# Band attention beside the convolution's products in the mixer of a first block, its values computed by token

## The reference, cut to what matters

```python
def first_block(x, ...):
    x = x + 0.5 * swiglu(rms_norm(x, ffn1_norm[l]), ...)
    h = rms_norm(x, mix_norm[l])
    proj = h @ w_in[l]                      # 1024 -> 3*512 + 512 + 8 + 8 + 3*512
    qkv_a, z_a, a_a, b_a, qkv_b = jnp.split(proj, split_at, axis=-1)
    o_a = gdn_mixer(qkv_a, z_a, a_a, b_a, conv_w[l], a_log[l], dt_bias[l], gdn_norm_w[l])
    o_b = dilated_mixer(qkv_b, q_norm_w[l], k_norm_w[l], rel_bias)
    x = x + jnp.concatenate([o_a, o_b], axis=-1) @ w_out[l]
    ...
def gdn_mixer(qkv, z, a, beta_logit, ...):
    qkv = jax.nn.silu(short_conv(qkv, conv_w))          # 5 taps along the tokens
    q, k, v = l2_normalize(qkv[0]), l2_normalize(qkv[1]), qkv[2]
    ...                                                 # delta rule, forward and backward
    o = rms_norm(o, norm_w) * jax.nn.silu(z)
def dilated_mixer(qkv, q_norm_w, k_norm_w, rel_bias):   # 8 heads of 64
    q = rms_norm(qkv[:, :, 0], q_norm_w) * (SWA_HEAD_DIM ** -0.5)
    k = rms_norm(qkv[:, :, 1], k_norm_w)
    v = qkv[:, :, 2]
    ...   # three dilations: band softmax of q k + bias, merged by their log sums
```

## Time and profile before

| | us |
|---|---|
| median of 3 runs (2813.7 to 2827.72) | 2822.07 |
| profiled execution | 2823.88 |
| its span | 2822.1 |
| PE busy in the span | 2644.0 (94%) |
| DVE busy | 1724.8 (61%) |
| ACT busy | 1046.6 (37%) |
| share of PE in the chain that ended last | 88% |

### The profile page before, as it was taken

One profiled execution on the slowest core, in us unless ns is written; L12 is line 12 of the kernel. 1 busy time (PEld: TensorE's weight loads), 2 busy tenths in 40 slices (PEclk: granted clock), 3 DMA queues, 4 the chain that ended last, 5 costly groups with the idle time before them and its releaser, 6 DMA issues.

```text
span 2822.1 us, 37400 instructions
## 1 busy us (share of the span) xinstructions
PE 2644.0 (94%) x15172; PEld 2280.8 (81%) x15172; DVE 1724.8 (61%) x2714; ACT 1046.6 (37%) x1575; POOL 135.6 (5%) x105
## 2 busy tenths in 40 slices
PE   7998879899799998998999999998999989898998
PEld 7998659899688887766878788887888877698898
DVE  5767474576676656455665666656555455586654
ACT  5445422444422223333243422223222224345543
POOL 0000013000000000032010000000000000310000
PEclk9999879899899999999999999999999999999999
DMA  7764200376355544211223255544343333154554
GB/s 239 233 226 177 75 1 1 124 237 221 113 177 181 174 148 139 72 34 54 93 84 103 91 185 174 173 155 132 120 145 129 125 116 97 49 158 149 164 186 144
DMA packets 110108, 380.90 MB, mean 135 GB/s; under 512 B 12016, under 2 KB 17392, under 8 KB 109552
## 3 DMA queue, kind: packets, MB, share of 16 engines
q1 hardware_dynamic: 108928, 373.32, 41.0%
q10 hardware_dynamic: 1008, 5.18, 0.5%
HBM read 377.40 MB, written 1.05 MB: 134 GB/s over the span
## 4 chain that ended last, share of the span: by engine, by line
PE 88%; DVE 7%; ACT 3%; issue 1%; POOL 0%; DMA 0%; SPq 0%; DVEq 0%; ACTq 0%
PE B L1195 25%; PE B L1196 25%; PE B L1197 25%; PE B L1411 2%; PE B L1210 1%; DVE w_lo L1717 1%; PE B L1211 1%; PE B L1212 1%; PE B L1427 1%; ACT w_hi L1480 1%; PE B L1335 1%; PE B L1321 1%; PE B L1328 1%; PE B L1418 1%; DVE TMP L1741 0%
## 5 line engine op out<-in xcount | busy, mean ns | idle before, releaser
L1195 PE MATMUL B<-U,w_hi 128*128 128x256 f32 (+1 forms) x2896 | 965.3, 333 | 13.1 <-DVE w_lo L1717 9.3
L1196 PE MATMUL B<-U,w_hi 128*128 128x256 f32 (+1 forms) x2896 | 957.9, 331 | 0.0
L1197 PE MATMUL B<-U,w_lo 128*128 128x256 f32 (+1 forms) x2896 | 957.8, 331 | 0.0
L1717 DVE TENSOR_TENSOR w_lo<-w_raw,w_hi 128x1024 fp32r<-128x1024 f32 (+3 forms) x587 | 683.9, 1175 | 438.7 <-ACT w_hi L1480 437.9
L1480 ACT ACTIVATE w_hi<-w_raw 128x1024 fp32r<-128x1024 f32 (+3 forms) x587 | 591.8, 1012 | 552.2 <-PE B L1197 527.0
L1195 PEld LDWEIGHTS B<-U,w_hi 128*128 128x128 f32 x2896 | 550.0, 190 | 70.6 <-issue 16.0
L1196 PEld LDWEIGHTS B<-U,w_hi 128*128 128x128 f32 x2896 | 548.1, 189 | 54.8 <-issue 2.1
L1197 PEld LDWEIGHTS B<-U,w_lo 128*128 128x128 f32 x2896 | 548.0, 189 | 52.8
L1195 PE MATMUL B<-HHf,w_hi 128*128 128x256 f32 (+1 forms) x1056 | 352.0, 333 | 0.0
L1196 PE MATMUL B<-HLf,w_hi 128*128 128x256 f32 (+1 forms) x1056 | 352.0, 333 | 0.0
L1197 PE MATMUL B<-HHf,w_lo 128*128 128x256 f32 (+1 forms) x1056 | 352.0, 333 | 0.0
(11 more groups left out here) (319 smaller groups left out, 2541.2 us busy)
## 6 DMA issues: line engine op xcount, KB each, us to landing
w_raw<-in_w SPq DMA_DIRECT2D x504, 512.0 KB, 4.2
w_ada<-in_w SPq DMA_DIRECT2D x144, 512.0 KB, 3.5
w_raw<-in_w SPq DMA_DIRECT2D x58, 384.0 KB, 3.2
w_raw<-in_w SPq DMA_DIRECT2D x16, 240.0 KB, 2.6
X<-in_x SPq DMA_DIRECT2D x2, 1024.0 KB, 9.7
w_raw<-in_w SPq DMA_DIRECT2D x8, 256.0 KB, 3.1
BW<-in_bias ACTq DMA_DIRECT2D x1, 1536.0 KB, 10.3
K<-in_consts ACTq DMA_DIRECT2D x2, 640.0 KB, 4.1
```

Source lines behind the costliest of these rows:

```text
L1195: pe.matmul(o, hi, xh, start=i == 0, stop=False)
L1196: pe.matmul(o, hi, xl, start=False, stop=False)
L1197: e = pe.matmul(o, lo, xh, start=False, stop=i == last)
L1717: dve.tensor_tensor(w_lo[:, plan.slot[u], 0:n], w_raw[:, plan.ring[u], 0:n], w_hi[:, plan.slot[u], 0:n].bitcast(F32), ALU.subtract).then_i ...
```

## The change

The list of generators gets another order. The attention's queries and keys 0 and 4 and all its values come right behind the first two products; each pair of heads starts as soon as its own query and key tile are there (before: all eight, and all values). The remaining products of the convolution stand between, and the gates come last.

The values are computed by token: the activations are the stationary operand and the weights move, 512 columns at a time, so the result has tokens in partitions and needs no transposes. SiLU of the convolution and of the gates is taken for four tiles at once; the taps add up in CQ itself, and the gates are copied to ZG first. The bias is prepared in eight pieces, one for each head, and a head waits for its own. The mixer's outputs go to the other half of U's tiles ("UO"), so they don't wait for the products that read the input.

```diff
-            b = self.gemm(("wout", m), [("wout", k, 128 * m, 128) for k in range(8)], 256, need=tuple(
+            b = self.gemm(("wout", m), [("wout", k, 128 * m, 128) for k in range(8)], 256, x="UO", need=tuple(
...
-            yield from TM.room()
-            t = TM.get()
-            self.add("conv_taps", key=j, t=t)
-            yield
-            self.add("conv_out", key=j, t=t, need=(old,))
-            TM.done(t, ("conv_out", j))
+            self.add("conv_taps", key=j, need=(old,))
+            yield
             done.add(j)
+
+        def conv_silu(g):
+            while not set(range(4 * g, 4 * g + 4)) <= done:
+                yield
+            self.add("conv_silu", key=g)
+            yield
+            silued.add(g)
 
         def gates(h):
             yield from PS.room()
             b = self.gemm(("in", 12 + h), win(128 * (12 + h)), 256)
-            yield
-            self.add("gdn_gate", key=h, b=b)
-            PS.done(b, ("gdn_gate", h))
+            self.add("gate_in", key=h, b=b, need=(old,))
+            PS.done(b, ("gate_in", h))
+            if h == 3:
+                yield
+                self.add("gate_silu")
...
         def unit(c):
-            while not {2 * c, 2 * c + 1} <= done:
+            while c // 2 not in silued:
                 yield
...
-            while len(qk) < 4 or len(done) < 12:
+            while 2 not in silued if base == 8 else len(qk) < 4:
                 yield
...
+        def attn_v():
+
             yield from PS.room(2)
...
+            b, b2 = PS.get(), PS.get()
+            self.add("v_mm", wts=self.weights([("win", k, 3088, 512) for k in range(8)]), b=b, b2=b2)
+            self.lastU = ("mm", "v")
+            for i, place in enumerate((b, b2)):
+                self.add("v_out", key=i, b=place, need=(old,))
+                PS.done(place, ("v_out", i))
+            yield
+            vb.append(1)
 
         def band(c):
-            while len(qn) < 8 or len(vb) < 4:
+            while not {c, 4 + c} <= qn or not vb:
                 yield
...
-            self.add("band_out", key=c, b=o, need=(self.lastU,))
+            self.add("band_out", key=c, b=o, x="UO")
...
-        tasks = [conv(0), conv(1)]
-        for j in range(2, 12):
-            tasks.append(conv(j))
-            if j < 10:
-                tasks.append(attn_v((j - 3) // 2) if j % 2 else gates((j - 2) // 2))
-        tasks.append(decay())
-        for j in range(8):
-            tasks.append(attn_qk(j))
-            if j % 2:
-                tasks.append(unit(j // 2))
-        tasks += [by_token(i, b, d) for i in range(2) for b, d in ((4, "K"), (8, "V"))]
-        tasks += [band(c) for c in range(4)]
+        tasks = [conv(0), conv(1), attn_qk(0), attn_qk(4), attn_v(), conv(2), band(0), conv(3), attn_qk(1), attn_qk(5),
+                 band(1), conv(4), conv(5), conv(6), conv(7), conv_silu(0), conv_silu(1), attn_qk(2), attn_qk(6), band(2),
+                 *[unit(c) for c in range(4)], conv(8), conv(9), attn_qk(3), attn_qk(7), band(3), decay(), conv(10), conv(11),
+                 *[gates(h) for h in range(4)], conv_silu(2)]
+        tasks += [by_token(i, b, d) for b, d in ((4, "K"), (8, "V")) for i in range(2)]
...
+    HI["UO"], LO["UO"] = HI["U0"][:, :, 256:512], LO["U0"][:, :, 256:512]
...
+            elif k == "v_mm":
...
+                for j, wt in enumerate(s.wts):
+                    hi, lo = weight(wt)
+                    w.wait_ge(*ready(wt[0]))
+                    for i, o in enumerate((PS(s.b), PS(s.b2))):
+                        x = slice(128 * i, 128 * i + 128)
+                        pe.matmul(o, HI[s.x][:, j, x], hi, start=j == 0, stop=False)
+                        pe.matmul(o, HI[s.x][:, j, x], lo, start=False, stop=False)
+                        e = pe.matmul(o, LO[s.x][:, j, x], hi, start=False, stop=j == 7)
...
-                w.wait_ge(*at("qk_out", 7))
+                w.wait_ge(*at("qk_out", c))
+                w.wait_ge(*at("qk_out", 4 + c))
...
+            elif k == "conv_silu":
+                v = CQ[:, 4 * s.key:4 * s.key + 4, :]
+                for j in range(4 * s.key, 4 * s.key + 4):
+                    w.wait_ge(*at("tap", (j, 4)))
+                act.activation(v, v, ACT.Silu).then_inc(*up("conv_silu", s.key))
...
-                pool.tensor_tensor(BW[:], BW[:], amask.unsqueeze(1).broadcast_to([128, 8, 384]),
-                                   ALU.add).then_inc(*up("bias", 0))
+                for h in range(8):
+                    pool.tensor_tensor(BW[:, h], BW[:, h], amask, ALU.add).then_inc(*up("bias", h))
```

More of the change, by code:

```diff
@@ L645, in finish @@
             yield
-            self.add("fin_out", key=c, t=t, t2=t2, need=(self.lastU,))
+            self.add("fin_out", key=c, t=t, t2=t2, x="UO")
             TM.done(t2, ("fin_n", c))
@@ L1251, in tensor @@
                 pe.matmul(PS(s.b, 256), bd, TM(s.t, 256), start=True, stop=True).then_inc(*up("qk_mm", s.key))
-            elif k == "v_tr":
-                w.wait_ge(*at("v_in", s.key))
+            elif k == "v_mm":
                 w.each(s.b.after)
-                for i in range(2):
-                    e = pe.transpose(hs(PS(s.b), i), hs(TM(s.t), i), ident)
-                e.then_inc(*up("v_tr", s.key))
+                w.each(s.b2.after)
+                for j, wt in enumerate(s.wts):
[6 more added lines that the diff above has]
+                        e = pe.matmul(o, LO[s.x][:, j, x], hi, start=False, stop=j == 7)
+                    if wt[3]:
+                        e.then_inc(*up("mm", ("unit", wt[0]), *["v"] * (j == 7)))
             elif k == "band_qk":
                 h, c, p = s.key, s.key // 2, 64 * (s.key % 2)
-                w.wait_ge(*at("qk_out", 7))
+                w.wait_ge(*at("qk_out", c))
+                w.wait_ge(*at("qk_out", 4 + c))
                 w.each(s.b.after)
@@ L1522, in scalar @@
                 w.wait_ge(*at("cv_pad", 1))
-                w.each(s.t.after)
-                act.activation(TM(s.t, 256), CV[:, s.key, 0:256], ACT.Copy,
+                w.each(s.need)
+                act.activation(CQ[:, s.key, :], CV[:, s.key, 0:256], ACT.Copy,
                                scale=col("conv_w", 5 * s.key)).then_inc(*up("tap0", s.key))
-            elif k == "conv_out":
-                w.wait_ge(*at("tap", (s.key, 4)))
+            elif k == "conv_silu":
[3 more added lines that the diff above has]
+                act.activation(v, v, ACT.Silu).then_inc(*up("conv_silu", s.key))
+            elif k == "gate_in":
+                w.wait_ge(*at("mm", ("in", 12 + s.key)))
                 w.each(s.need)
-                act.activation(CQ[:, s.key, :], TM(s.t, 256), ACT.Silu).then_inc(*up("conv_out", s.key))
-            elif k == "gdn_gate":
-                w.wait_ge(*at("mm", ("in", 12 + s.key)))
-                act.activation(ZG[:, s.key, :], PS(s.b, 256), ACT.Silu).then_inc(*up("gdn_gate", s.key))
+                act.activation(ZG[:, s.key, :], PS(s.b, 256), ACT.Copy).then_inc(*up("gate_in", s.key))
+            elif k == "gate_silu":
+                w.wait_ge(*at("gate_in", 3))
+                act.activation(ZG[:], ZG[:], ACT.Silu).then_inc(*up("gate_silu", 0))
             elif k == "decay_exp":
@@ L1544, in scalar @@
             elif k == "l2_sq":
[L1545 removed]
+                w.wait_ge(*at("conv_silu", s.key // 2))
                 w.each(s.t.after)
@@ L1563, in scalar @@
                 act.activation(TM(s.t2, 256), TM(s.t2, 256), ACT.Exp, scale=-0.5).then_inc(*up("qk_exp", s.key))
-            elif k == "v_in":
-                w.wait_ge(*at("mm", ("v", s.key)))
-                w.each(s.t.after)
-                act.activation(TM(s.t, 256), PS(s.b, 256), ACT.Copy).then_inc(*up("v_in", s.key))
             elif k == "v_out":
-                w.wait_ge(*at("v_tr", s.key))
+                w.wait_ge(*at("mm", "v"))
                 w.each(s.need)
-                act.activation(VB[:, :, 128 * s.key:128 * s.key + 128], band2(PS(s.b, 256)),
-                               ACT.Copy).then_inc(*up("v_out", s.key))
+                act.activation(VB[:, s.key, :], PS(s.b), ACT.Copy).then_inc(*up("v_out", s.key))
             elif k == "band_exp":
@@ L1799, in vector @@
             elif k == "conv_taps":
-                j, o = s.key, TM(s.t, 256)
+                j, o = s.key, CQ[:, s.key, :]
                 w.wait_ge(*at("tap0", j))
@@ L1849, in vector @@
                 w.wait_ge(*at("band_qk", h))
-                w.wait_ge(*at("bias", 0))
+                w.wait_ge(*at("bias", h))
                 w.each(s.t.after)
```

25 lines of the change are left out of this document (5 added, 20 removed).

## The result

Measured side by side on one chip, the changed kernel takes 2799.39 us (median of 9 runs, 2792.47 to 2807.61), the kernel before 2818.21 (9 runs, 2807.85 to 2827.72): ratio 0.9933, 95% interval 0.9917 to 0.995. That is 18.8 us, 0.7%: small, but outside the noise.

The account below looks back on a forecast made before the run. TensorE was taken as nearest to a bound, with 62 of the mixer stretch's 169.8 us lost. 108 us of work plus 37.8 of remaining losses gave 145.8, 24.0 less: 2798 us, own case 2788 to 2808, range 2779 to 2816.

Parts of the forecast that it names:

- work at full clock: TensorE's products, values, heads, sums and transposes in the first block's mixer, priced from matmul counts at 108 us.
- front: Mixer start while GpSimd prepares the bias: eight pieces and work in hand remove TensorE's 8.81 us wait, cost 0.
- sums of squares: Eight sums over attention queries and keys each wait 0.47 us for ScalarE's square: 3.8 us.
- first head: TensorE waits between the first head's scores and transposes, with only two products to cover taps, exponential, split and normalization: 3 us.
- scores of heads 2, 4, 6: These scores stand right behind a key's sum and wait for that key's normalization, 2.2 us three times: 6.6 us.
- around head 3: Table loads and SiLUs around head 3's exponential delay its transposes by 3.9 us and the next query's square by 0.8: 4.7.
- four sums in a row: Sums over the convolution's queries and keys, with no product between, leave TensorE waiting for ScalarE: 5 us.
- clock at the decay: The fall behind the decay's short matmuls stays, 7 us at 0.51: 3.4 us.
- delta rule's entry: Delta rule begins with the same inputs and distances: 0, up to 3 us if TensorE enters at the lower clock.
- the low clock: Rival: with heads among products, TensorE's clock falls at the first head and stays low, 26 us lost, 2848 us; 5%.
- The front's stall: Rival: eight bias pieces hold VectorE as long as one did and TensorE runs out, 9 us lost, 2807 us; 10%.
- the exposed heads: Rival: every head exposes the first one's wait, seven more times 2.5 us, 17.5 lost, 2815 us; 15%.

Follow-up runs that it names:

- e1: Changed kernel with the four pairs of heads moved to the end of the list, behind the transposes to token order: 2810.73 us, 0.9972 of the kernel before.
- e2: Changed kernel with the bias prepared in one GpSimd instruction instead of eight pieces: 2804.16 us, 0.9947 of the kernel before.
- e5: Kernel before with one edit, the bias prepared in eight GpSimd pieces, one for each head: 2813.85 us, 0.998 of the kernel before.
- e11: Changed kernel with the decay's 48 short matmuls moved later, behind the second gate: 2795.8 us, 0.9935 of the kernel before.
- e6: Changed kernel with the four sums over convolved queries and keys placed apart, between products: 2798.24 us, 0.9926 of the kernel before.
- e9: Changed kernel with the two SiLUs over the convolution's queries and keys directly behind one another in one step: 2799.64 us, 0.9952 of the kernel before.
- e4: The changed kernel measured again with no edit, as a yardstick: 2804.86 us, 0.9947 of the kernel before.

## Why the prediction held, point by point

The predicted terms against the trace of after, in us:

| term | predicted | measured |
|---|---|---|
| work at full clock | 108 | 115.4 |
| start at the lower clock | 2.7 | 2.3 |
| front | 0 | 0 (0.5 for the constants, in the next row) |
| sums of squares | 3.8 | 0.9 |
| first head | 3 | 1.8 |
| scores of heads 2, 4, 6 | 6.6 | 5.8 |
| around head 3 | 4.7 | 3.7 (2.40 + 1.26) |
| four sums in a row | 5 | 2.9 |
| other heads | 0 | 1.5 (0.8 transposes, 0.7 output) |
| clock around 280 to 300 | 5 | 3.8 |
| clock at the decay | 3.4 | 6.8 |
| end | 3.6 | 3.9 |
| sum | 145.8 | 148.8 |

Nearly every loss was at its place, and its engine and instruction were the ones named; the mechanism was right, and e1, e2 and e5 bear it out. The exception is the row of sums of squares: eight waits were priced, and outside head 3 only one came, with the half microsecond for the constants. Two sizes were off and all but cancelled, which is luck: 7.4 us too little work and 1.8 too little clock against 6.2 too much waiting.

The time was luck too. From profile to profile the kernel became 24.5 us shorter, where 24.0 were forecast; but only 17.8 of them come from the change, and 6.7 from a stage that happened to be slow in the profile of before. The nine runs of before less the forecast gain would be 2794 us.

The work term: 108 from counts, 115.4 measured. The trace of before could have told it: 169.8 less 28.9 of standing and 24.7 of clock is 116.2, and the change hardly touches the work. Part of the error is a misreading of the earlier trace rows. The number behind the x counts the matmuls that touch the 10 us, not those that start in them: 91 touch the 10 us from 550, and 88 start there; of those with 512 columns 46 touch the 10 us from 900, and 44 start there. The rest is that a product hands over to what follows. Starts of after, a product with a product behind it, and one with scores behind it:

```profile
214.74 0.28 PE L1205 MATMUL B<-U,w_hi 128*128 128x256 f32 x1
...
217.46 0.28 PE L1190 MATMUL B<-U,w_hi 128*128 128x256 f32 x1
...
236.27 0.28 PE L1190 MATMUL B<-U,w_hi 128*128 128x256 f32 x1
...
239.10 1.13 PE L1265 MATMUL B<-QB 64*128 64x256 f32 x4
240.15 0.39 PE L1190 MATMUL B<-U,w_hi 128*128 128x256 f32 x1
```

The first takes 217.46 - 214.74 = 2.72 us, 0.113 a matmul instead of 0.110; the second 239.10 - 236.27 = 2.83. The twenty products of after that run wholly at 1.00 take 2.90 in the mean, 0.25 more than priced, 6 us for 24. The values take 11.2 (225.09 to 236.27) instead of 10.4. A head's scores take 1.05, its transposes 0.50 and its output 1.01 (from their starts), 2.56 instead of 2.4, 1.3 for eight. Together these are 8 us, slightly more than the 7.4 missing.

The other error went the other way: the waits were taken as if nothing else stood before them, 26.7 us in sum (3.8 + 3 + 6.6 + 4.7 + 5 + 3.6) against 20.5. Around head 3 the sum itself slips: its terms, 1.28 + 1.04 + 1.28 + 0.9 + 1.65 less one product of 2.65, give 3.5 and not 3.9 (2.40 measured).

The decay's clock: priced with the 7 us of before; it became 14, and why is open (e11). The delta rule's entry, put at 0 with up to 3 us allowed, took 3.2. The front held, though for more than the reason given: e2 shows that what stands there covers 6.5 us even with one long instruction. The pieces cost GpSimd more than 0.86 us each: 10.91 in all, and each split of weights beside them 1.6 to 2.0 instead of 1.22.

```profile
224.90 10.91 POOL L2105 TENSOR_TENSOR BW<-BW,CB 128x384 f32<-128x384 f32 x8 [20.90 <-DMA BW<-in_bias]
...
229.38 1.62 DVE L1719 TENSOR_TENSOR w_lo<-w_raw,w_hi 128x1024 fp32r<-128x1024 f32 x1 [0.33 <-ACT w_hi L1482]
```

The table is loaded six times, each 1.28 us, as said (columns: start, duration; four of them around head 3):

```profile
270.98 0.51 ACT L1526 ACTIVATE CQ<-CV,PC 128x256 f32<-128x256 f32 x1
271.51 1.28 ACT L1532 ACT_TABLE_LOAD   x1
272.80 1.06 ACT L1532 ACTIVATE CQ<-CQ 128x1024 f32<-128x1024 f32 x1
273.88 1.28 ACT L1461 ACT_TABLE_LOAD   x1
...
276.10 1.28 ACT L1532 ACT_TABLE_LOAD   x1
...
280.17 1.28 ACT L1461 ACT_TABLE_LOAD   x1
```

The Trainium skill, "ScalarE: Activation LUTs", section "What ACT_TABLE_LOAD costs", makes its 2.7 us of about 1.28 for the load and 1.38 for a drain. The trace agrees with the first and shows nothing of the second: the instruction ahead of the load ends at 271.49, and the one behind it starts at 272.80.

Of the rivals, the low clock (the heads at 0.50 among products too) is refuted by 245 to 270 at 1.00. The prediction let a rule on transposes stand for whole heads; a head is also scores and an output, 2.06 of its 2.56 us, so the stretch at 0.50 does not single out the transposes. The front's stall and the exposed heads did not come. The signs named beforehand are there: scores of the first head at 239.10, the first delta matmul at 358.52 (356 forecast), waits of 1.77 us before the first head's transposes (3) and 2.40 before the fourth's (4).

## What to carry to other kernels

Before a stage is priced by counts, cut it into standing, clock and work from its own trace: the work that a reordering leaves alone is then known, and only the other two are open. Small dependent chains are better placed among long products than in a row: in this kernel that gave the clock's part of the gain and about half of the standing's (e1). A wait removed is a gain only if the queue behind it is ready: e6 took away 2.5 us of waits and got 1.7 back at the next ones and the rest from the clock, e9 took away two table loads and found the whole wait at the next instruction.

## What the runs showed of the hardware that was not expected

The same code runs at two paces at a granted clock of 1.00. Here are the first network's products at 100 to 110 us, which no kernel here changes, in the profiles of after and of e4, which are one program:

```profile
100.00:110.00 10.00, 10.00 (x91) 10.00 (x90) 7.74 (x13) 5.41 (x8) 0.00 (x0) 1.00 0.67 229
```

```profile
100.00:110.00 10.00, 10.00 (x87) 10.00 (x86) 7.76 (x11) 4.41 (x8) 0.00 (x0) 1.00 0.49 172
```

91 matmuls of 256 columns touch this stretch against 87, with starts 0.113 or 0.118 us apart, and PE is busy in both. A stage of some 200 us is then 6.5 to 7.5 us longer, and it sets in for whole stages at a time: the mixer starts at 209.7 or at 216.5, the second block takes 203.8 or 210.6, the last stage 187.5 or 194.8. In e4's profile all three were slow, which accounts for the 20.1 us by which its span is longer than after's; in that of before only the last was. For the runs without a profile (2793.82 to 2819.54 us in e4's twelve) it is the likely reason of the spread, not a shown one; its cause was not sought.

Whether the clock falls can hang on little: 250 to 270 had 0.83 in e2 and 1.00 in after, with 18.2 and 18.4 us of PE busy in 20. Such a fall is worth some 3 us, as much as most edits tried here. It need not be chance: the three profiles of the changed kernel all have 1.00 there, and e2 has one profile.

An instruction of GpSimd can hold up one of VectorE nearly to its own end: one addition of 6.84 us stretches a 0.59 us multiplication to 6.53 (e2). Eight pieces take 10.39 to 10.91 in all, with VectorE's longer as well. How much of that is VectorE holding GpSimd and how much each piece's own cost was not separated; the shortest piece takes 1.0 us, the longest 2.0, where an eighth of 6.84 is 0.86.
